# A two-layer hybrid trunk on one core: K tiles between units, transposes a step later, banks emptied ahead of weight halves, loads in parts

## The reference

```python
def _layer(x, ...):
    proj = jnp.einsum('btd,de->bte', x, w_in)
    hq, hf, hi, hg, rq, rk, rv, rg, su = jnp.split(proj, cuts, axis=-1)
    f_gate = lbf + (1.0 - lbf) * jax.nn.sigmoid(hf)
    o_hg, s_hg_new = _chunked_gated_linear(silu(hq), (1 - lbf) * sigmoid(-hf), hi, log(f_gate), s_hg)
    o_hg = head_rms_norm(o_hg) * hg_norm_w * silu(hg)
    o_rt, s_rt_new = _chunked_gated_linear(rotary(rq), rotary(rk) * RET_DK ** -0.5, rv, log_gamma, s_rt)
    o_rt = head_layer_norm(o_rt) * ret_norm_w * silu(rg)
    y5, s_re_new, s_im_new = _s5_scan(su, ...)          # complex diagonal state space, 16 groups
    y5 = gelu(y5); y5 = y5 * sigmoid(y5 @ s5_glu_w + s5_glu_b)
    mixed = concatenate([o_hg, o_rt, y5]) @ w_out
    x = layer_norm(ALPHA * x + mixed)
    ff = square(relu(x @ w_up)) @ w_down
    x = layer_norm(ALPHA * x + ff)
    return x, s_hg_new, s_rt_new, s_re_new, s_im_new
```

## Time and profile before

| | us |
|---|---|
| median of three runs | 741.53 |
| lowest, highest | 739.55, 748.14 |
| profiled execution | 747.85 |
| its span, first to last instruction | 746.1 |
| PE busy | 716.9 (96%) |
| DVE, ACT, POOL busy | 536.8, 411.5, 40.6 |
| mean granted clock of PE | 0.982 |

### The profile page before, as it was taken

The page is one execution under the profiler, slowest core; times in us unless marked ns, Lnnn a source line. Parts: engine busy times, 40 slices in busy tenths (PEclk is TensorE's granted clock), DMA queues, the critical chain, the costliest instruction groups (busy, mean ns, idle before and its releaser), DMA issues. The chain is left out here.

```text
span 746.1 us, 17512 instructions
## 1 busy us (share of the span) xinstructions
PE 716.9 (96%) x7224; PEld 661.0 (89%) x7224; DVE 536.8 (72%) x969; ACT 411.5 (55%) x771; POOL 40.6 (5%) x54
## 2 busy tenths in 40 slices
PE   8999899999999999999989999999999999999994
PEld 7788768869999999999979887877999999999993
DVE  7978864378787988874775987556878776555474
ACT  5533043456687566773558423365568755677342
POOL 1100102100000000000040002020000000000001
PEclk9999898999999999999999999999999999999998
DMA  7831124436465555565524312342636555655531
GB/s 257 306 115 59 60 86 159 168 97 193 136 194 171 181 189 186 180 184 156 178 78 141 96 51 86 132 152 62 221 116 200 185 179 178 188 174 190 177 113 58
DMA packets 30718, 112.50 MB, mean 151 GB/s; under 512 B 3536, under 2 KB 3744, under 8 KB 30256
## 3 DMA queue, kind: packets, MB, share of 16 engines
q1 hardware_dynamic: 28080, 100.78, 42.7%
q0 software_dynamic: 1984, 9.54, 3.5%
q10 hardware_dynamic: 576, 1.08, 0.4%
HBM read 107.20 MB, written 4.18 MB: 149 GB/s over the span
## 5 line engine op out<-in xcount | busy, mean ns | idle before, releaser
L1629 DVE TENSOR_TENSOR w_low<-w_raw,w_high 128x1024 fp32r<-128x1024 f32 x161 | 197.0, 1224 | 113.0 <-ACT w_high L1146 111.1
L1146 ACT ACTIVATE w_high<-w_raw 128x1024 fp32r<-128x1024 f32 x161 | 170.4, 1058 | 150.0 <-PE stream L1086 135.5
L1084 PE MATMUL stream<-a_high,w_high 128*128 128x264 f32 x520 | 155.0, 298 | 3.1 <-DVE a_low L2239 3.0
L1085 PE MATMUL stream<-a_low,w_high 128*128 128x264 f32 x520 | 149.1, 287 | 0.0
L1086 PE MATMUL stream<-a_high,w_low 128*128 128x264 f32 x520 | 148.9, 286 | 0.0
L1084 PE MATMUL stream<-h_high,w_high 128*128 128x264 f32 x512 | 146.3, 286 | 0.0
L1086 PE MATMUL stream<-h_high,w_low 128*128 128x264 f32 x512 | 145.1, 283 | 0.0
L1085 PE MATMUL stream<-h_low,w_high 128*128 128x264 f32 x512 | 145.0, 283 | 0.0
L1084 PEld LDWEIGHTS stream<-a_high,w_high 128*128 128x128 f32 x520 | 99.5, 191 | 8.1 <-issue 5.7
L1085 PEld LDWEIGHTS stream<-a_low,w_high 128*128 128x128 f32 x520 | 99.7, 192 | 0.4
L1086 PEld LDWEIGHTS stream<-a_high,w_low 128*128 128x128 f32 x520 | 99.3, 191 | 0.0
(11 more groups left out here) (394 smaller groups left out, 995.8 us busy)
## 6 DMA issues: line engine op xcount, KB each, us to landing
w_raw<-in_weights SPq DMA_DIRECT2D x190, 512.0 KB, 3.6
mats<-in_matrices POOLq DMA_DIRECT2D x2, 1024.0 KB, 7.6
S_hg<-in_state_hg POOLq DMA_DIRECT2D x2, 768.0 KB, 5.9
out_hg_s<-S_hg POOLq DMA_DIRECT2D x2, 768.0 KB, 3.7
consts<-in_constants POOLq DMA_DIRECT2D x1, 1499.5 KB, 6.5
X<-in_xT ACTq DMA_DIRECT2D x4, 264.0 KB, 5.1
out_y<-X SPq DMA_DIRECT2D x4, 264.0 KB, 2.1
S_rt<-in_state_rt POOLq DMA_DIRECT2D x2, 512.0 KB, 6.7
```

The costliest lines, as they stand in the source:

```text
L1084: pe.matmul(bnk[:, 0:width], wh, xh, start=(first and kk == 0), stop=False)
L1085: pe.matmul(bnk[:, 0:width], wh, xl, start=False, stop=False)
L1146: act.activation(w_high[:, SPLIT_SLOT[n], :], w_raw[:, RAW_SLOT[n], :], ACT.Copy).then_inc(high_ready, 1)
L1629: put(tt(w_low[:, SPLIT_SLOT[n], :], w_raw[:, RAW_SLOT[n], :], w_high[:, SPLIT_SLOT[n], :].bitcast(F32), ALU.subtract), low_ready)
```

## The change

- `IDLE_PRODUCTS` goes from 5 to 4.
- POOL loads in parts. `mats` comes in four pieces of 512 columns (256 KB each) under semaphores `c_loaded`, `bt_loaded` and `mats_loaded` (B and `glu`): C behind weight block 2, BT in POOL's step 6, B and `glu` in step 11. The constants are laid out anew, so that `decay` and `k_decay` stand last: 951 columns come in step 5, `decay` in step 13, `k_decay` in 14. Masks and `s5x0` come in step 8, `S_hg` in 10, `S_rt` in 14. POOL's step k waits until k - 2 products of whole blocks are done. In layer 1 the same pieces come one after the other where `mats` came. Readers wait for their own piece.
- Layer 0: the transposes `tr_hi 0`, `tr_hi 1`, `tr_hi_sample`, `tr_hk_sample` move from step 11 to 12; ACT copies them in its step 13.
- Layer 0: `STOPS` puts `s5_in_sample` behind K tile 3 and level 3 behind K tile 5 of step 13, and level 4 behind K tile 4 of step 14.
- Layer 0: `ret_score 4` and `5` stand first among the units of step 18.
- DVE, layer 0: `level_decay 5` stands later in step 13, behind `s5_half` and `s5_sample_states`; `hgrn_sample_add 2` in step 18 and `ret_scores 4, 5` in step 19 stand ahead of the halves. Layer 1: `near_level 0` in step 9 stands ahead of the half.

The diff, cut:

```diff
@@ -80,7 +80,7 @@
...
 for _name, _n in (("ident", 128), ("head_mean", 128), ("model_mean", 128), ("cos", T), ("sin", T),
-                  ("decay", HEADS * 256), ("k_decay", 512), ("gamma", 2), ("eps", 1), ("pair_sum", BLOCK), ("quad_sum", 4), ("steps", S5_CHUNKS)):
+                  ("gamma", 2), ("eps", 1), ("pair_sum", BLOCK), ("quad_sum", 4), ("decay", HEADS * 256), ("k_decay", 512), ("steps", S5_CHUNKS)):
     CV[_name] = (_at, _n)
@@ -115,13 +115,14 @@
...
     _plan((13, 5)[_l], ("s5_in_sample",), layers=(_l,))
+_plan(18, ("ret_score", 4), ("ret_score", 5), layers=(0,))
 for _l in range(DEPTH):
...
         _plan(8 + _s + _r, *[("hg_level", _r, _h) for _h in range(2)], layers=(_l,))
-    _plan(11, ("tr_hi", 0), ("tr_hi", 1), ("tr_hi_sample",), ("tr_hk_sample",), layers=(_l,))
+    _plan((12, 11)[_l], ("tr_hi", 0), ("tr_hi", 1), ("tr_hi_sample",), ("tr_hk_sample",), layers=(_l,))
     _plan((13, 5)[_l], ("s5_out", 0), layers=(_l,))
@@ -134,8 +135,9 @@
...
     _plan(17 + _s, ("hg_o", 0), ("hg_o", 1), ("hg_o", 2), ("hg_state",), layers=(_l,))
-    _plan(18, ("tr_rv_sample",), ("tr_rk_sample",), ("tr_rv", 0), ("tr_rv", 1), ("ret_score", 4), ("ret_score", 5), layers=(_l,))
+    _plan(18, ("tr_rv_sample",), ("tr_rk_sample",), ("tr_rv", 0), ("tr_rv", 1), layers=(_l,))
     _plan((22, 19)[_l], ("hg_ms",), layers=(_l,))
+_plan(18, ("ret_score", 4), ("ret_score", 5), layers=(1,))
 _plan(20, ("ret_kv", 0), ("ret_kv", 1), ("ret_o", 0), ("ret_o", 1), ("ret_o", 2), ("ret_state",))
@@ -156,7 +158,7 @@
...
     _plan(N_CHUNKS - 1, *[("s5_tab_near", _l + 1, _h) for _h in range(2)], layers=(_l,))
-STOPS = ({19: (3, 6), 21: (4,), 22: (2, 5, 6, 7), UP_A + 1: (3, 5)}, {17: (3, 6), 21: (4,), 22: (2, 4, 6), UP_A + 1: (3, 5)})
+STOPS = ({13: (3, 5), 14: (4,), 19: (3, 6), 21: (4,), 22: (2, 5, 6, 7), UP_A + 1: (3, 5)}, {17: (3, 6), 21: (4,), 22: (2, 4, 6), UP_A + 1: (3, 5)})
 UNITS_OF = {"s5_out": lambda u: [], 
@@ -196,7 +198,7 @@
...
 DECAY_AT = ({1: 10, 2: 11, 3: 11, 4: 12, 5: 13, 6: 14, 7: 15}, {r: 7 + r for r in range(1, 8)})
-IDLE_PRODUCTS = 5
+IDLE_PRODUCTS = 4
 
@@ -530,7 +533,37 @@
...
                 pool.dma_start(S_hg[:, :, :, :], state_hg[l]).then_inc(states_loaded, 16)
-                pool.dma_start(S_rt[:, :, :, :], state_rt[l]).then_inc(states_loaded, 16)
+
+            def load_states_rt(l):
+                pool.dma_start(S_rt[:, :, :, :], state_rt[l]).then_inc(rt_loaded, 16)
+
+            def load_constants(a, b, loaded):
+                pool.dma_start(consts[:, a:b], constants[:, a:b]).then_inc(loaded, 16)
+
+            def load_matrices(l, a, b, loaded):
+                pool.dma_start(mats[:, a:b], matrices[l, :, a:b]).then_inc(loaded, 16)
+
+            def first_loads(k):
+
+                early = CV["decay"][0]
+                decays = CV["k_decay"][0]
+                if k == 5:
+                    load_constants(0, early, const_loaded)
+                elif k == 6:
+                    load_matrices(0, 1536, MATS, bt_loaded)
+                elif k == 8:
+                    pool.dma_start(masks[:, :, :], level_masks).then_inc(const_loaded, 16)
+                    pool.dma_start(s5x0[:, :, :, :, :], state_s5).then_inc(const_loaded, 16)
+                elif k == 10:
+                    load_states(0)
+                elif k == 11:
+                    load_matrices(0, 0, 512, mats_loaded)
+                    load_matrices(0, 1024, 1536, mats_loaded)
+                elif k == 13:
+                    load_constants(early, decays, decay_loaded)
+                elif k == 14:
+                    load_constants(decays, CV["steps"][0], decay_loaded)
+                    load_states_rt(0)
 
@@ -555,11 +588,7 @@
...
             wait_raw(pool, 2)
-            pool.dma_start(mats[:, :], matrices[0]).then_inc(mats_loaded, 16)
-            wait_raw(pool, 4)
-            pool.dma_start(consts[:, 0:a], constants[:, 0:a]).then_inc(const_loaded, 16)
-            pool.dma_start(masks[:, :, :], level_masks).then_inc(const_loaded, 16)
-            pool.dma_start(s5x0[:, :, :, :, :], state_s5).then_inc(const_loaded, 16)
+            load_matrices(0, 512, 1024, c_loaded)
             def clear_mixers():
@@ -567,16 +596,15 @@
...
             for l in range(DEPTH):
-                if l == 0:
-                    pool.wait_ge(chunk_done, 6)
-                    load_states(0)
-                else:
+                if l:
                     pool.wait_ge(chunk_done, l * N_CHUNKS)
...
                     s = LATER[l]
+                    if l == 0:
+                        first_loads(k)
                     if 14 + s <= k <= 16 + s:
@@ -603,12 +631,16 @@
...
                     pool.wait_ge(table_ready, l + 1)
-                    pool.dma_start(mats[:, :], matrices[l + 1]).then_inc(mats_loaded, 16)
+                    load_matrices(l + 1, 512, 1024, c_loaded)
+                    load_matrices(l + 1, 1536, MATS, bt_loaded)
+                    load_matrices(l + 1, 0, 512, mats_loaded)
+                    load_matrices(l + 1, 1024, 1536, mats_loaded)
                     pool.wait_ge(outs["hg_s"], 16 * (l + 1))
...
                     load_states(l + 1)
+                    load_states_rt(l + 1)
                 centre()
@@ -1270,7 +1303,7 @@
...
                     copied(ustep_ready, l + 1, fu)
-                if c == 12:
+                if c == (13, 12)[l]:
                     act.wait_ge(table_ready, l + 1)
@@ -1988,7 +2024,7 @@
...
                 for r in range(1, 8):
-                    if l == 0 and c == DECAY_AT[l][r]:
+                    if l == 0 and r != 5 and c == DECAY_AT[l][r]:
                         level_decay(l, r)
@@ -2001,9 +2037,9 @@
...
 
-                if c == FIRST_LEVEL[l] + 1:
+                if l == 0 and c == FIRST_LEVEL[l] + 1:
                     near_level(l, 0)
-                if 14 + s <= c < (17 + s, 16)[l]:
+                if 14 + s <= c < 16 + s:
                     hgrn_sample_add(l, c - 14 - s)
@@ -2012,7 +2048,7 @@
...
                 for r in range(1, 8):
-                    if l and c == DECAY_AT[l][r]:
+                    if (l or r == 5) and c == DECAY_AT[l][r]:
                         level_decay(l, r)
@@ -2043,7 +2079,7 @@
...
                         ret_k_decay(l, t)
-                if 17 <= c < 20:
+                if 17 <= c < (19, 20)[l]:
                     for h in range(2):
@@ -2268,6 +2304,13 @@
...
                     n = l * N_CHUNKS + c
+                    if l == 0 and c == 18:
+                        hgrn_sample_add(l, 2)
+                    if l == 0 and c == 19:
+                        for h in range(4, 6):
+                            ret_scores(l, h)
+                    if l and c == FIRST_LEVEL[l] + 1:
+                        near_level(l, 0)
                     if l and c in (6, 7):
```

11 lines of the change are left out of this document (8 added, 3 removed).

## The result

Both kernels were timed on the same chip, 20 runs each. The changed kernel takes **736.93 us** (median, 734.57 to 741.89), the kernel before 741.63 us (738.94 to 748.14): a ratio of 0.9935, with a 95% interval of 0.9914 to 0.9957, so 4.7 us or 0.65% less. The forecast was 735.9 us. The profiled execution of the changed kernel took 739.92 us, with a span of 738.1 us; it is one of the longer ones, as that of before was.

The account below looks back on a forecast made before the run. TensorE, busy 96% of the span, was taken as the bound. Terms -1.8 + 0.6 - 1.7 - 0.9 - 1.2 = -5.0 us, with -0.6 for the clock, took 741.5 to 735.9 us; 8-in-10 range 731.0 to 741.0.

Parts of the forecast that it names:

- if DVE is late for more than the transposes: One of three signs, to be looked for in the profile after, that would show the forecast wrong.
- Loads, -1.8 us: Layer 0, steps 2 to 14: step 4's 1.7 us weight-block wait goes, one idle product fewer gains 0.1 us.
- Transposes, +0.6 us: Steps 11 to 12: 0.96 us of bank waits go, new waits of about 0.8 and 0.75 us come.
- K tiles, -1.7 us: Steps 13 and 14: the 2.8 us "issue" wait, read as for code, goes; 1.05 us may remain.
- rival D: Step 14: the 2.83 us wait is not for code and stays; 737.6 us, chance 0.06.
- Banks, -0.9 and -1.2 us: Banks emptied ahead of halves: ret_score's wait in layer 0 step 17, and level 1's in layer 1 step 9, shrink.
- The clock, -0.6 us: Two half-clock stretches after steps with idle PE: the median run is allowed 1.2 us of loss, half of which goes.
- 1.00 between 80 and 115 us: Expected sign in the profile after: granted clock at full speed throughout that stretch.
- Rival B: Waits only change place: code waits at both packets, transposes cost +1.5, hg_kv 2's bank no sooner; 739.3 us, chance 0.18.
- Rival C: Slower: step 12's two transpose waits halve the clock at about 74 us, step 14's keeps it; 743.3 us, chance 0.05.
- Rival A: The clock counts in full: the median run has both half-clock stretches and they go; 731.6 us, chance 0.24.
- T1: Theory at the experiments' start: each part is worth its term, terms add up, what is missing is clock.

Follow-up runs that it names:

- the second pair: Changed kernel with sample add 1 ahead and six unused products between layers: transposes back in step 11, 736.92 us, against not put back, 733.95 us.
- add 1 ahead: Changed kernel with sample add 1 also ahead of step 18's weight half on VectorE: 734.63 us, ratio 0.9915.
- wait filled: Changed kernel with sample add 1 ahead, plus six unused products in TensorE's wait between the layers: 733.95 us, ratio 0.9888.

## Why the prediction was right, and where it was not

The time came within 1.0 us of the forecast, and the mechanisms that it named are in the trace. The terms, though, were right in part only, and that the sum came out so well is luck: the errors have both signs. By its own signs the forecast was wrong in one thing, "if DVE is late for more than the transposes": it was, by 1.54 us in step 16. Medians below are against the changed kernel's 736.93 and 736.70 us.

**Loads, -1.8 us.** Right where it was worked out: step 11 starts 1.78 us earlier than before (table), and undoing the part costs 1.8 to 1.9 us there. Even the wait in step 7 of the kernel with the old loads follows from the same count (the block issued at 25.00 us landed at 33.16, 8.2 us against 7.2). Wrong was to carry it to the end: 0.1 to 0.3 us in the median, about 1 us by the ratios, neither clear of noise.

**Transposes, +0.6 us.** The two waits were 0.59 and 1.13 us, 1.72 together, where I had 0.8 and 0.75, 1.55. As TensorE's own delay the term was about right: step 13 starts 0.96 us later than with the transposes as before, 0.8 of it from this part. As the part's worth in time its sign is most likely wrong: undoing it makes the kernel 1.5 to 2.3 us slower, and in the second pair 2.8 to 3.0, with overlapping intervals both times and with more half clock in both. I had counted what TensorE waits, and had noted that VectorE would be free of the moved decay, but had not asked what the order does to VectorE: it gets `s5_in 1` 1.06 us earlier, and it is the engine that steps 13 to 16 hang on. This is the step that failed; the runs show the 1.06 us and 0.92 us of it at the start of step 17.

**K tiles, -1.7 us.** The reading of the wait as one for code is borne out: it comes back when the K tiles are whole, and moves by 64 instructions when 64 are put ahead. The 1.05 us that I left in the level of step 14 were 0, 0.50, 0 and 1.05 us in four executions with the same TensorE code up to there (the changed kernel twice, add 1 ahead, wait filled), and 0 in two more (loads and banks as before). Where there was a wait it stood at the product that the count of 240 instructions gives, and it ended 2.4 to 2.6 us behind the start of an instruction packet. The term was too small in the company of the other parts (3.9 to 4.4 us) and not to be told from zero by itself (-0.1% for the cut in the kernel before, with an interval from -2.9 to +1.5 us). By the rule of "Instruction fetch mechanics" in the Trainium skill's "Runtime: NRT & Kernel Launch", a mostly hidden crossing, rival D would hold; the 2.81 and 2.83 us speak against it in this one place, though most of the 57 packets are waited for by nobody.

**Banks, -0.9 and -1.2 us.** Layer 1: 0.26 us are left, as predicted, and undoing gives 1.40 us. Step 17: the wait is gone, but whether by this part is open. It did not come back without the part, in an execution whose half clock in step 17 gave VectorE 1.7 us to catch up.

**The clock, -0.6 us.** "1.00 between 80 and 115 us" was wrong for the first profile and right for the second. The median half clock did not fall by what can be told (17.6 and 13.2 us, before 13.3 to 19.3). Over the 20 runs of the changed kernel the time rises by 0.48 us for each us of half clock, so this makes up most of its spread of 7.3 us.

**Rival B** had the right mechanism at 0.18: "a PE that comes earlier meets" VectorE. It happened, for 1.54 us, in step 16, which no term of mine looked at. Its other three conditions did not hold. Rival C's condition, two waits among the transposes that bring the clock down at about 74 us, occurred in one execution (72.2 us), for 3.4 us instead of 13.6. Rival A needed both half-clock stretches gone; in each profile of the changed kernel one was there ahead of 110 us.

**Not additive.** The parts undone singly cost 3.9, 0.1, 1.5 and 2.1 us, 7.6 in all (8.3 by the ratios), for a gain of 4.7; and the largest of them alone gives nothing measurable, so T1 does not hold as it stands. Only the first of the four is clear of noise. As far as that goes, the parts need each other: cutting the K tiles brings TensorE forward, and VectorE must be brought forward too for it to count. That is argued from the traces; no run has two of the parts alone.

What stays open: why an instruction packet starts later in one execution than in another of the same code, so that an "issue" wait of 0.5 to 1.05 us comes in steps 9 to 16, what the add in front gains in step 17, why the clock falls behind the same waits in some executions only, and how much of the gain of the add and of the filled wait is real beyond the overlap of their intervals with that of the changed kernel.

## What to carry to other kernels

Before adding up what a change takes off the busiest engine, follow the second engine through the same steps: where it has no idle time, what feeds it earlier counts, and a wait that you remove elsewhere comes back at the next bank it empties. Ask for each unit that is moved who is given work sooner, not only who waits. And let the edit that mends one wait (an add ahead of a weight half) be tried at its neighbours of the same form; here the next one took 1.3 us off a wait, where the first one's share could not be told.
